# Four RMS norms of a two-block transformer kernel: the inverse roots are applied after the projections instead of before the turning

## The reference

```python
def rmsnorm(x, g):
    y = xf * lax.rsqrt(jnp.mean(xf * xf, axis=-1, keepdims=True) + EPS)
    return y * g
h = h + 0.5 * swiglu(rmsnorm(h, ffn1_norm), w_gate, w_up, w_down)   # silu(x @ w_gate) * (x @ w_up) @ w_down
u, v, z, xbc, dt_raw = split(rmsnorm(h, mix_norm) @ w_in)           # gated spatial mixing and a state-space mixer
h = h + concatenate([ya, yb]) @ w_out
h = h + 0.5 * swiglu(rmsnorm(h, ffn2_norm), ...)
gate = sigmoid(rmsnorm(h, ple_norm) @ ple_w_gate + ple_b_gate)
h = h + gate * (p @ ple_w_proj)
return rmsnorm(h, final_norm)
```

## Time and profile before

| | us |
|---|---|
| median of 3 runs (lowest, highest) | 1831.54 (1829.39, 1831.86) |
| the profiled execution | 1831.15 |
| its span | 1829.4 |
| TensorE busy | 1709.1 (93%) |
| VectorE busy | 1262.3 (69%) |
| ScalarE busy | 919.7 (50%) |

### The profile page before, as it was taken

One profiled execution on the slowest core, in us unless ns is written; L12 is line 12 of the kernel. 1 busy time (PEld: TensorE's weight loads), 2 busy tenths in 40 slices (PEclk: granted clock), 3 DMA queues, 4 the chain that ended last, 5 costly groups with the idle time before them and its releaser, 6 DMA issues.

```text
span 1829.4 us, 32109 instructions
## 1 busy us (share of the span) xinstructions
PE 1709.1 (93%) x13106; PEld 1539.4 (84%) x13106; DVE 1262.3 (69%) x2043; ACT 919.7 (50%) x1238; POOL 83.4 (5%) x49
## 2 busy tenths in 40 slices
PE   6898787998989999999999999899998998999996
PEld 6676577998988888999999999799988777799985
DVE  5886655899889999777775555655555886555555
ACT  3455545554445554454454554544445765644445
POOL 1100003531000000000000000000000000000000
PEclk9899888999989999999999999999998998999998
DMA  7653223444434445554554555345553532555541
GB/s 269 265 183 119 101 104 119 159 163 161 141 115 145 156 142 205 203 190 171 202 194 174 203 188 185 138 184 185 184 164 125 207 136 95 190 185 185 185 163 68
DMA packets 45365, 304.02 MB, mean 166 GB/s; under 512 B 5057, under 2 KB 5217, under 8 KB 11298
## 3 DMA queue, kind: packets, MB, share of 16 engines
q1 hardware_dynamic: 44034, 295.92, 45.0%
q0 software_dynamic: 1184, 6.05, 0.8%
HBM read 299.83 MB, written 2.13 MB: 165 GB/s over the span
## 4 chain that ended last, share of the span: by engine, by line
PE 63%; DVE 26%; ACT 7%; issue 2%; DMA 1%; DVEq 0%; SPq 0%; ACTq 0%
PE pb L825 62%; DVE ar L1740 8%; DVE w_lo L1740 7%; ACT ar L1319 3%; DVE ar L1752 2%; ACT w_hi L1319 2%; ACT L1319 1%; DVE HC L1740 1%; DVE ar L2086 1%; DMA raw<-in_wall 1%; DVE ar L1889 1%; DVE ar L2083 1%; DVE raw L1889 1%; DVE ar L1886 1%; DVE ar L1756 0%
## 5 line engine op out<-in xcount | busy, mean ns | idle before, releaser
L1740 DVE TENSOR_TENSOR w_lo<-raw,w_hi 128x1024 fp32r<-128x1024 f32 x467 | 573.2, 1227 | 306.2 <-ACT w_hi L1319 285.2
L825 PE MATMUL pb<-HX,w_hi 128*128 128x256 f32 x3904 | 717.2, 286 | 8.1 <-DVE w_lo L1740 7.8
L1319 ACT ACTIVATE w_hi<-raw 128x1024 fp32r<-128x1024 f32 x498 | 528.2, 1061 | 299.4 <-PE pb L825 281.3
L825 PEld LDWEIGHTS pb<-HX,w_hi 128*128 128x128 f32 x3904 | 618.5, 194 | 14.5 <-DVE w_lo L1740 6.8
L825 PE MATMUL pb<-HX,w_lo 128*128 128x256 f32 x1952 | 555.5, 285 | 0.0
L825 PE MATMUL pb<-w_hi,HC 128*128 128x512 f32 (+1 forms) x1648 | 530.5, 393 | 0.4 <-DVE HC L1752 0.4
L825 PEld LDWEIGHTS pb<-HX,w_lo 128*128 128x128 f32 x1952 | 377.7, 193 | 0.0
L825 PEld LDWEIGHTS pb<-w_hi,HC 128*128 128x128 f32 x1648 | 311.0, 189 | 63.5 <-DVE HC L1752 0.8
L825 PE MATMUL pb<-w_lo,HC 128*128 128x512 f32 (+1 forms) x824 | 321.3, 390 | 0.0
L1740 DVE TENSOR_TENSOR ar<-ar 128x512 bf16<-128x512 bf16 (+8 forms) x470 | 268.5, 608 | 62.9 <-ACT ar L1319 42.7
L1319 ACT ACTIVATE ar<-pb 128x512 f32<-128x512 f32 (+2 forms) x237 | 135.7, 573 | 252.3 <-PE pb L825 197.7
(11 more groups left out here) (131 smaller groups left out, 720.5 us busy)
## 6 DMA issues: line engine op xcount, KB each, us to landing
raw<-in_wall SPq DMA_DIRECT2D x257, 1024.0 KB, 4.8
ar<-in_wmod SPq DMA_DIRECT2D x24, 512.0 KB, 3.6
x<-in_wmod SPq DMA_DIRECT2D x8, 512.0 KB, 3.4
ar<-in_bigrows POOLq DMA_DIRECT2D x2, 1024.0 KB, 5.0
ar<-acs_keep POOLq DMA_DIRECT2D x2, 1024.0 KB, 6.1
ar<-in_crow SPq DMA_DIRECT2D x2, 512.0 KB, 5.9
x<-in_x SPq DMA_DIRECT2D x1, 1024.0 KB, 10.4
ar<-in_ctx SPq DMA_DIRECT2D x1, 1024.0 KB, 14.3
```

The costliest lines, as they stand in the source:

```text
L825: return e.matmul(o, l, r, start=start, stop=stop, skip_group_check=True)
L1319: a.did(e.activation(out, in_, func, scale=scale, **kw), sig)
L1740: v.did(e.tensor_tensor(out, a_, b_, op), sig)
```

## The change

It leaves `N_PEER` as it was (`turn_normed`, `normed`, `normed_highs`, `normed_lows` are its former parts) and rewrites the four later norms:

- TensorE transposes `x` itself, with the identity, not a scaled diagonal. Both tiles of a block land side by side in one bank (`rows_bank`), so high and low halves are made for both tiles at once, in 8 operations of 256 columns on each engine in place of 16 of 128. Blocks 0 to 3 of tile 0 are turned ahead of the last two units of the second sweep, and everything else after it (`turn_rest`).
- ScalarE splits its weights ahead of the first squares, and the squares of tile 1 come after the high halves. VectorE makes both inverses after the low halves.
- In the feed-forward stages a row of inverse roots in all partitions (`inv`) is made by two matmuls of a matrix of ones with `dgn` behind the first gate product (`inverse_rows`); VectorE multiplies every gate product by it before Silu, which then reads SBUF and stands behind the splitting for the up units in ScalarE's list. The up product stays unscaled: its factor comes in at the end, where `halved` uses half the inverse root in place of 0.5.
- In the mixer the copy of the `xbc` products becomes a product with `inv`, `dt` and the token-major activations take the inverse root as a scale, and so does the last gate.
- Some semaphores are merged, and GpSimd sets the matrix of ones during the expert layer.

```diff
+        def rows_bank(k):
+            return PB[k // 4 * 2 + k % 2][:, k // 2 % 2 * 256:k // 2 % 2 * 256 + 256]
@@ last_four, second sweep @@
-                    if n == 3 and j != N_END:
-                        turn_rows(j, 0)
+                    if n == 3 and j == N_PEER:
+                        turn_normed(0)
+                    if n == 2 and j in (N_F1, N_MIX, N_F2, N_PLE):
+                        t.wait_ge(s_res, result(j, 0, 1))
+                        turn_rows(0, range(4))
+            def turn_rows(i, ks):
+                for k in ks:
+                    ins = e.transpose(rows_bank(k)[:, i * 128:(i + 1) * 128], x[:, i, k * 128:(k + 1) * 128], ident)
+                    if i:
+                        t.did(ins, s_nt)
+            def turn_rest(j):
+                t.wait_ge(s_res, result(j, 1, 0))
+                turn_rows(1, range(4))
+                t.wait_ge(s_res, result(j, 1, 1))
+                for k in range(4, 8):
+                    turn_rows(0, [k])
+                    turn_rows(1, [k])
+            def inverse_rows(j):
+                t.wait_ge(s_set, 2)
+                t.wait_ge(s_nd, 4 + 2 * j + 2)
+                t.wait_ge(s_nl, both_turned(j, 2))
+                for i in range(2):
+                    ins = mm(PB[0][:, i * 128:(i + 1) * 128], ones, dgn[:, i, :], True, True)
+                t.did(ins, s_inv)
 # ffn and mixer on TensorE: turn_rows(j, 1) becomes turn_rest(j), and
+                        if c == p == 0:
+                            inverse_rows(j)
 # the last gate
-        GT_BANK = [0, 1, 6, 7]
+        GT_BANK = [6, 7, 0, 1]
+                if i:
+                    t.wait_ge(s_nl, both_turned(N_PLE, max(k, 3)))
 # ScalarE
             def norm(j, last, scr_):
+                ahead(last - 2)
+                ahead(last - 1)
+                squares(j, 0, scr_)
                 ahead(last)
                 if j == N_PLE:
...
-                highs(j, 1)
+                for k in range(8):
+                    a.wait_ge(s_nt, both_turned(j, k // 4 * 4 + 2 + k % 2))
+                    if k >= 2:
+                        a.wait_ge(s_nl, both_turned(j, k - 2))
+                    act(HX[:, 0, k, :], rows_bank(k), ACT.Copy, scale=norm_gain(j, k), sig=s_nh, free=True)
+                squares(j, 1, scr_)
 # ffn on ScalarE
-                    a.wait_ge(s_used, used(at[0] + 1))
-                    if c > 1:
-                        a.wait_ge(s_ml, n0 + c - 1)
-                    act(f_sg[:, c % 2, :], PB[BK[c % 2][0]][:, :], ACT.Silu, sig=s_sg)
                     for m in range(2):
                         ahead(at[1] + m)
+                    a.wait_ge(s_gr, n0 + c + 1)
+                    act(f_sg[:, c % 2, :], f_sg[:, c % 2, :], ACT.Silu, sig=s_sg)
 # VectorE
             def norm(j, last, add):
                 v.wait_ge(s_t0, j + 1)
                 add(0)
                 ahead(last - 2)
                 ahead(last - 1)
+                v.wait_ge(s_used, used(last))
+                add(1)
+                for k in range(8):
+                    v.wait_ge(s_nh, both_turned(j, k))
+                    stt(HX[:, 1, k, :], rows_bank(k), norm_gain(j, k), HX[:, 0, k, :].bitcast(F32), MUL, SUB, sig=s_nl,
+                        free=True)
+                ahead(last)
+                for i in range(2):
+                    inverse(j, i)
+                ts(half_inv, root_, 0.5)
 # gate_up on VectorE, after the gate product's two units
+                    if c == 0:
+                        inverse_rows(2 if n0 else 0)
+                    v.wait_ge(s_used, used(at[0] + 1))
+                    tt(f_sg[:, c % 2, :].rearrange("p (m t) -> p m t", m=2),
+                       PB[BK[c % 2][0]][:, :].rearrange("p (m t) -> p m t", m=2), bc(inv, 1, 2), MUL, sig=s_gr)
-                    stt(xx, PB[2 * i + hf][:, :], 0.5, xx, MUL, ADD, sig=s_res, free=True)
+                    stt(xx, PB[2 * i + hf][:, :], half_inv[:, i:i + 1], xx, MUL, ADD, sig=s_res, free=True)
-                cp(xbT[:, 2 * c:2 * c + 2, 4:260], PB[4 + c % 2][:, :].rearrange("p (a b) -> p a b", a=2), sig=s_xb)
+                tt(xbT[:, 2 * c:2 * c + 2, 4:260], PB[4 + c % 2][:, :].rearrange("p (a b) -> p a b", a=2), bc(inv, 1, 2), MUL,
+                   sig=s_xb)
```

More of the change, by code:

```diff
@@ L1185, in tensor_program @@
             ffn(U_FFN1, N_F1, 0)
-            turn_rows(N_MIX, 1)
+            turn_rest(N_MIX)
             for c in range(6):
@@ L1195, in tensor_program @@
                 if c == 0:
+                    inverse_rows(N_MIX)
                     t.wait_ge(s_dw, 1)
@@ L1386, in norm @@
-            def norm(j, last, scr_):
-                squares(j, 0, scr_)
+                    if k % 2:
+                        a.wait_ge(s_nt, bank_turned(i, k))
+                        if 8 * i + k >= 4:
+                            a.wait_ge(s_nl, 8 * i + k - 3)
+                        act(scaled4[:, k % 4, :], norm_bank(i, k), ACT.Identity, scale=G2[:, k:k + 1],
+                            bias=modT[:, 24 + k, 0:1])
+                    else:
+                        a.wait_ge(s_nf, 4 * i + k // 2 + 1)
@@ L1389, in norm, with normed @@
+                    act(norm_half(0, i, k), scaled4[:, k % 4, :], ACT.Copy, sig=s_nh)
+            def normed(last, scr_):
+                squares(N_PEER, 0, scr_)
                 ahead(last - 2)
                 ahead(last - 1)
-                if j == N_PEER:
-                    highs(j, 0, range(2))
-                    squares(j, 1, scr_)
-                    highs(j, 0, range(2, 8))
-                else:
-                    highs(j, 0)
-                    squares(j, 1, scr_)
+                normed_highs(0, range(2))
+                squares(N_PEER, 1, scr_)
+                normed_highs(0, range(2, 8))
+                ahead(last)
+                normed_highs(1, range(8))
@@ L1398, in norm @@
+            def norm(j, last, scr_):
+                ahead(last - 2)
+                ahead(last - 1)
+                squares(j, 0, scr_)
                 ahead(last)
@@ L1516, in scalar_program @@
             ahead(U_OUT1 + 4)
-            norm(N_PEER, U_OUT1 + 7, scr3)
+            normed(U_OUT1 + 7, scr3)
             def scores_out(c):
@@ L2072, in vector_program @@
             ahead(U_OUT1 + 4)
-            norm(N_PEER, U_OUT1 + 7, lambda i: gated(i, gate, yo1))
+            normed(U_OUT1 + 7, lambda i: gated(i, gate, yo1))
             def top16(jobs):
@@ L2236, in gate_up @@
                     at = ffn_at(base, c)
-                    for p in range(2):
-                        for m in range(2):
-                            ahead(at[p] + m)
+                    for m in range(2):
+                        ahead(at[0] + m)
+                    if c == 0:
[3 more added lines that the diff above has]
+                       PB[BK[c % 2][0]][:, :].rearrange("p (m t) -> p m t", m=2), bc(inv, 1, 2), MUL, sig=s_gr)
+                    for m in range(2):
+                        ahead(at[1] + m)
                     v.wait_ge(s_sg, n0 + c + 1)
@@ L2476, in gpsimd_program @@
             p.wait_ge(s_w, 24)
+            p.did(e.memset(ones, 1.0), s_set)
             gate_row(1, gate5)
```

174 lines of the change are left out of this document (80 added, 94 removed).

## The result

| | before | changed kernel |
|---|---|---|
| median, us (lowest, highest), 4 runs each | 1831.31 (1829.39, 1831.86) | 1810.30 (1807.33, 1811.93) |
| ratio, 95% interval | | 0.9885 [0.9868, 0.9902] |
| profiled execution, us | 1831.15 | 1811.93 |
| its span | 1829.4 | 1810.2 |

The gain is 21.0 us between the medians, 19.2 us between the profiled executions. 16.7 us had been forecast (1814.5), with 1808.0 to 1825.5 as the range.

A forecast was written before the change was run, and what follows sets the result against it. TensorE, busy 1709.1 of 1829.4 us, was taken as the bound, with the gain at four norms. Stretch gains of 21.2 less 1.5 for ones and 3.0 for the clock gave 16.7 us: 1814.5 us, range 1808 to 1825.5.

The forecast's parts named there:

- The four stretches: First addition to the next projection's first matmul at each later norm: gains of 7.5, 5.4, 4.9 and 3.4 us.
- The price of a unit: The projection's first unit, 24 matmuls, taken as 2.9 us, half of 6.03 us for 48 with rounding.
- That the roots are the reason: The root of tile 1 stands in the middle of each norm's stretch, 69.2 us in all, and the change removes it.
- The root that still stands in front at `N_MIX`: At the mixer's norm a root not needed there stands ahead of the high halves on ScalarE; cost 0.9 us.
- The added matmuls of ones: `inverse_rows` on TensorE costs 0.5 us at three norms, 1.5 us in all, without a wait.
- The product on the gate: VectorE's added product in 22 feed-forward chunks, 0.69 us each, 15 us in all, lies beside TensorE; cost 0.
- The table load without a drain: First table load at a norm priced at 1.28 us; an added drain of about 1.38 would make the sum 13.9.
- The clock: Slow TensorE time may fall on the projection, none or 1.5 us at each norm; 3 us taken over four.
- no slow stretch at all: Rival: idle time at the norms is too short to lower TensorE's clock; 1809.5 us, chance 0.17.
- The mixer: Sign of being wrong: the mixer, where VectorE and ScalarE are dense, gives back what its norm won.
- The last gate: At `N_PLE` the stretch falls to 17.8 us, ending with the split the last gate waits for; gain 3.4 us.

The follow-up runs named there:

- e1: The changed kernel with tile 1's squares, both inverses and the turning after the sweep waiting for the roots again at the four later norms: 1820.45 us, ratio to before 0.9944.
- e7: The changed kernel with the third split of weights behind both roots at the norm before the mixer: 1812.25 us.
- e2: The changed kernel without the 22 products of the gate with the inverse roots, Silu reading PSUM at its old place: 1810.98 us, ratio to before 0.9904.
- e9: The changed kernel computing only the first of dt's 8 blocks, 6 matmuls of 16 columns in place of 48: 1802.28 us, one run.
- e10: The changed kernel with dt's product turned round, 24 matmuls of 256 columns and then 6 of 16 in place of 48: 1801.55 us, one run.
- e4: The changed kernel with the last gate's first splits ahead of the high halves and two more ahead of tile 1's squares at `N_PLE`: 1802.91 us, ratio 0.9853.
- e6: The kernel before, with only dt's 48 small matmuls moved behind the second pair of the mixer's units: 1822.39 us, ratio 0.9973, ten runs in two groups.
- e12: The changed kernel with dt's 48 small matmuls behind the second pair of the mixer's units instead of the first: 1803.16 us, ratio to before 0.9852.

## Why the prediction was right

- *Where the gain lies.* The four norms, by 18.0 of 19.2 us between the profiled executions. The four stretches were predicted at 10.5, 10.3, 9.4 and 17.8 and came out at 10.54, 10.53, 9.34 and 17.64. The step that gave them, the order of ScalarE's list (two splits, squares, root, table load, split, high halves) and halves 0.50 us behind each other, holds row by row: two blocks took 1.01 to 1.09 us, but for 1.25 at the start of `N_F1` (1170.17 to 1171.42), where the first unit ends 0.5 us later than predicted. The price of a unit, 2.9 us, was taken from matmuls of 16 columns and from a sum of 6.03 us for 48 that the earlier trace rows does not show (it has 1.85 us for 16); that it fits the 24 matmuls of 256 columns (2.87 us for the second unit at `N_MIX`) was luck.
- *That the roots are the reason.* This is shown for less than half of the gain, 8.2 of 18.0 us. `e1` takes the gain back at `N_F2` (4.7 of 5.2 us) and half of it at `N_F1` (3.6 of 6.9). What is left for the other half there is turning with one record of a transpose in place of two, half the operations, and blocks turned before the sweep ends; they were not tried one by one. At `N_MIX` and `N_PLE` `e1` has the roots in front and keeps 3.3 of 3.5 and all of 2.5 us. So the prediction's picture, a root of tile 1 in the middle of each stretch, holds for the stretches of three norms, but only two stages are shorter by it.
- *The root that still stands in front at `N_MIX`,* priced at 0.9 us. It is there (the high halves start 8.43 us after the first addition, at `N_F2` 7.24), and `e7` removed 1.1 us of it. That it was worth 0.9 us of time was wrong: the mixer behind it shows no gain from it.
- *The added matmuls of ones,* 0.5 us at three norms. They take 0.59 us before the mixer and waited for nothing at any norm, as the prediction had it.
- *The product on the gate,* cost 0: `e2`.
- *The table load without a drain.* The changed kernel's root starts 1.30 us after the load here too (1360.38 to 1361.68), as in the earlier trace rows, and the split follows. The stretches by the Trainium skill's price of a switch (ScalarE: Activation LUTs, What ACT_TABLE_LOAD costs) would have been 1.4 us longer at `N_F1` and `N_MIX`; they were not.
- *The clock,* 3.0 us as the middle between none and 1.5 us a norm. This is the term that was sized wrongly, norm by norm and in the sum. Stage gain less stretch gain, without the 0.6 for the ones, gives what else was lost: nothing at `N_F1` (6.9 against 7.5 less 0.6), a win of 0.9 at `N_F2` (5.2 against 4.9 less 0.6), because there the projection before had started at half clock, a loss of 1.1 at `N_MIX` (0.4 by the mixer of `e2`) and of 1.0 at `N_PLE`. Net 1.2 us or less in place of 3.0. The rival "no slow stretch at all" is what happened at `N_F1` and `N_F2`; at `N_PLE` the slow matmuls lasted 5.0 us where they had lasted 2.9 in the kernel before, and in the mixer it is not the projection that was slow.
- *The mixer,* named as a place that might give back what its norm won. It gave back 1.7 of 5.2 us, or 1.0 by the mixer of `e2`. Ahead of the second pair the loss is larger, 0.6 for the ones and 1.9 for a longer dt, and some of it comes back further on. These are windows and rows of the kernel before:

```profile
1372.70:1382.70 10.00, 7.56 (x50) 7.59 (x51) 7.35 (x18) 7.94 (x18) 2.29 (x4) 0.83 0.62 247
1382.70:1387.70 5.00, 5.00 (x47) 5.00 (x45) 2.62 (x3) 3.66 (x6) 0.00 (x0) 1.00 0.59 210
1387.70:1397.70 10.00, 10.00 (x60) 10.00 (x61) 2.02 (x2) 1.16 (x2) 0.00 (x0) 0.66 0.33 107
```

```profile
1384.38 6.03 PE L825 MATMUL pb<-HC,HX 128*128 128x16 f32 x48
1390.26 0.77 PE L825 MATMUL pb<-HX,w_hi 128*128 128x256 f32 x2
```

  Before, the clock fell at the norm, where TensorE waited, was up again for most of the 48 matmuls of dt (6.03 us) and fell as they ended. Now nothing falls at the norm; the 48 take 7.97 us, since half clock sets in during them, and lasts to 1384. The second pair starts 24.8 us after the first addition in place of 27.6. `e1` and the changed kernel differ by 4.3 us at the norm (the first pair ends 20.7 and 16.3 us after the first addition). dt takes `e1` 2.4 us less, and the second pair 1.0 less, since 3.1 us of it run at half clock, against 5.1 in the changed kernel; so the second and the third pair's products come 0.9 us later in `e1`, and the stage ends 0.15 to 0.9 later. `e9` and `e10` show that the fall goes with the 48 small matmuls.
- *The last gate,* 3.4 us predicted, 2.5 measured. The stretch was right (3.5); more half clock behind a wait of 5 us took 1.0 of it. `e4` shows that the wait was a matter of order, worth 7.1 us.
- *The rest:* 16.7 us forecast, 18.0 in the stages: 1.8 more by the clock term, 0.3 less by the ones, 0.1 less by the stretches. Between 18.0 and the 21.0 of the medians lie the 1.2 us in unchanged code and the 1.6 from the profiled execution of the changed kernel, the slowest of its four, to their median. Both are of the size by which executions of one kernel differ, so part of the distance from 16.7 to 21.0 is chance, and so is how near the median comes to the rival's 1809.5: that rival's time needs a clock that stays up at all four norms, and at the last gate it did not.

## What to carry to other kernels

A factor that belongs to a row can be taken out of a chain of dependent steps and applied behind the product, wherever the engine that applies it has slack: the price is a few operations that another engine's work covers (here 15 us of VectorE, which cost nothing). The gain has to be looked for stage by stage: here the freed steps shortened two stages by 8.2 us, and at the other two norms something else was waited for. Then read what stands behind the freed place: here the next two limits, each about 7 us, were questions of order in a list (small matmuls ahead of products that a busy engine waits for, a split of weights queued behind halves), and each showed as one row with a wait or a window at half clock with TensorE 100% busy. A stage length tells edits apart that medians cannot, if its own scatter is known: it was 0.1 us for the first feed-forward stage and 0.7 for the mixer.

## What the runs showed that was not expected

- TensorE can lose its clock while the profile shows it busy without a gap. The clock fell during the 48 matmuls of 16 columns in every profile that has them; with 24 of 256 columns and 6 of 16, or 6 of 16 alone, in their place it did not. The Trainium skill (TensorE: Matmul & The Clock Gate, Part 4: PE-mode transpose) says that transposes do not bring the clock to full; here sixteen transposes at a norm, among matmuls and with the clock at full ahead of them, cost no clock, as the windows at `N_F1` and `N_F2` show. Whether they could bring it up no run here shows.
- A matmul of 16 columns takes about as long as one of 256: 5.58 / 48 = 0.116 us in `e1`, where the clock was at full for nearly all of them, and 2.98 / 24 = 0.124 in `e10`. The wide form does the same multiplications in half the number of matmuls, so it takes half the time at full clock. It yields dt with tokens in columns, and what turning that back costs was not tried.
- The same edit (dt later) gives two groups of times, 7 us apart, on the old norms (`e6`) and one group on the new ones (`e12`). What tells the groups apart stays open, and with it what the edit is worth on the old norms.
